# A hand-written order of a mixer's first inverses: chunks 0 and 1 first, convolutions in single steps

## The reference, cut to what matters

```python
S = S * w_t + sa (x) (kk_t * a_t) + v_t (x) k_t      # sa = S @ -kk_t; per token, 8 heads of 64
y = S @ r_t                                          # rwkv7_step, scanned over 512 tokens
...
xc = conv_b + sum(xp[:, i:i+seqlen] * conv_w[i] for i in range(4))
r, i_g = sigmoid(blocks(xc) @ gate_a_w + b), sigmoid(blocks(xc) @ gate_x_w + b)
a = exp(-8 * r * softplus(-lam)); u = sqrt(1 - a*a) * i_g * xc
h = scan(a, u); out = h * gelu(gb)                   # rglru_mix, 4 tiles of 128 channels
```

## Time and profile before

| | us |
|---|---|
| median of 3 runs | 3383.71 (3383.62 to 3385.1) |
| the profiled execution | 3382.94 |
| its span | 3381.2 |
| TensorE busy | 3325.3 (98%) |
| VectorE busy | 1982.3 (59%) |
| ScalarE busy | 1378.0 (41%) |
| GpSimd busy | 30.2 (1%) |

### The profile page before, as it was taken

One profiled execution on the slowest core, in us unless ns is written; L12 is line 12 of the kernel. 1 busy time (PEld: TensorE's weight loads), 2 busy tenths in 40 slices (PEclk: granted clock), 3 DMA queues, 4 the chain that ended last, 5 costly groups with the idle time before them and its releaser, 6 DMA issues.

```text
span 3381.2 us, 44358 instructions
## 1 busy us (share of the span) xinstructions
PE 3325.3 (98%) x18719; PEld 2691.3 (80%) x18719; DVE 1982.3 (59%) x2907; ACT 1378.0 (41%) x2111; POOL 30.2 (1%) x68
## 2 busy tenths in 40 slices
PE   8999999999999999999999999999999999999998
PEld 7888878888888888885788888657888887588887
DVE  6554687675546653436564435576765366676644
ACT  4332367443324332336543322365543243654433
POOL 0000003000000000000000000000000000000000
PEclk9999999999999999999999999999999999999999
DMA  5444430244443432220122223201223232023221
GB/s 199 144 144 148 132 119 3 94 148 140 142 150 125 157 111 94 90 100 32 38 94 98 96 99 144 69 32 57 98 97 100 92 143 69 13 82 105 95 100 56
DMA packets 93079, 342.32 MB, mean 101 GB/s; under 512 B 10320, under 2 KB 10832, under 8 KB 92368
## 3 DMA queue, kind: packets, MB, share of 16 engines
q1 hardware_dynamic: 92880, 339.48, 30.1%
HBM read 337.34 MB, written 2.10 MB: 100 GB/s over the span
## 4 chain that ended last, share of the span: by engine, by line
PE 89%; DVE 6%; ACT 4%; issue 1%; DMA 0%; POOL 0%; SPq 0%; DVEq 0%; ACTq 0%; POOLq 0%
PE ps L812 21%; PE ps L813 21%; PE ps L814 21%; PE ps L917 2%; PE ps L918 2%; PE ps L921 2%; PE ps L966 1%; PE ps L968 1%; PE ps L967 1%; PE ps L942 1%; PE ps L943 1%; PE ps L944 1%; ACT WK L2211 1%; DVE SPL L2320 1%; PE ps L1514 1%; ACT SPH L1607 1%
## 5 line engine op out<-in xcount | busy, mean ns | idle before, releaser
L2320 DVE TENSOR_TENSOR SPL<-RAW,SPH 128x1024 fp32r<-128x1024 f32 x522 | 635.6, 1223 | 876.6 <-ACT SPH L1607 876.2
L1607 ACT ACTIVATE SPH<-RAW 128x1024 fp32r<-128x1024 f32 x522 | 548.2, 1056 | 974.2 <-PE ps L814 867.4
L812 PE MATMUL ps<-HH,SPH 128*128 128x512 f32 x2312 | 910.2, 394 | 3.1 <-ACT WK L2138 1.9
L814 PE MATMUL ps<-HH,SPL 128*128 128x512 f32 x2312 | 900.2, 389 | 0.0
L813 PE MATMUL ps<-HL,SPH 128*128 128x512 f32 x2312 | 900.2, 389 | 0.0
L812 PEld LDWEIGHTS ps<-HH,SPH 128*128 128x128 f32 x2312 | 434.0, 188 | 104.8 <-issue 11.1
L813 PEld LDWEIGHTS ps<-HL,SPH 128*128 128x128 f32 x2312 | 434.1, 188 | 92.2 <-issue 3.6
L814 PEld LDWEIGHTS ps<-HH,SPL 128*128 128x128 f32 x2312 | 434.0, 188 | 90.7
L812 PE MATMUL ps<-AH,SPH 128*128 128x512 f32 x996 | 389.1, 391 | 0.7 <-DVE AH L2672 0.7
L814 PE MATMUL ps<-AH,SPL 128*128 128x512 f32 x996 | 387.7, 389 | 0.0
L813 PE MATMUL ps<-AL,SPH 128*128 128x512 f32 x924 | 359.6, 389 | 0.0
(11 more groups left out here) (570 smaller groups left out, 4335.2 us busy)
## 6 DMA issues: line engine op xcount, KB each, us to landing
RAW<-in_ws SPq DMA_DIRECT2D x522, 512.0 KB, 3.3
RAW<-in_wa SPq DMA_DIRECT2D x96, 512.0 KB, 3.5
WK<-in_sm SPq DMA_DIRECT2D x2, 2784.0 KB, 9.9
WK<-in_cst SPq DMA_DIRECT2D x2, 1664.0 KB, 7.5
X<-in_x SPq DMA_DIRECT2D x8, 256.0 KB, 8.2
out<-X SPq DMA_DIRECT2D x8, 256.0 KB, 2.7
WK<-in_sm SPq DMA_DIRECT2D x1, 768.0 KB, 4.9
PCT<-in_pc SPq DMA_DIRECT2D x1, 349.0 KB, 2.7
```

Of the source, the lines that this page charges most:

```text
L812: e.matmul(out, wh, rhs[0], start=start, stop=False)
L814: mm = e.matmul(out, wl, rhs[0], start=False, stop=stop)
L1607: e.activation(SPH[:, q:q + 1024], RAW[:, r:r + 1024], ACT.Copy).then_inc(hi_ready.did(("hi", n)))
L2320: e.tensor_tensor(SPL[:, q:q + 1024], RAW[:, r:r + 1024], SPH[:, q:q + 1024].bitcast(F32), ALU.subtract).then_inc(lo_ready.did(("lo", n)))
```

## The change

Chunk 0's `w0` moves from GpSimd to VectorE, as the new branch `w0`; the other three stay on GpSimd, chunk 1's now ahead of the memsets `t64`. On TensorE two `lt` are made first, then the values' transposes `vt` (before: after `nm` 3,3), then the first `nm` of chunks 0 and 1, with the other two `lt` between. `tr` 0 takes the place where `vt` was. `conv` takes a list of steps, and the three steps of tiles 0 and 1 stand as single items between the levels; tile 1's come behind tile 0's. On ScalarE `vtc` and `tanh` 0 move ahead, `gelu` behind `tanh` 0, and `bonb` behind `sq` 0; `kt` 0 and `bt` 0 move to where `vtc` was. The items behind those shown are as they were.

```diff
--- before.py
+++ after.py
@@ -196,14 +196,14 @@
 BONUS_SUMS_AT, BONUS_AT = {12: 0, 15: 1, 18: 2, 21: 3}, {13: 0, 16: 1, 19: 2}
 
 
-MIX0_TENSOR = [("01", "lt", 1), ("23", "lt", 0), ("45", "lt", 3), ("67", "lt", 2), ("23", "tr", 0),
-               ("0", "nm", 0, 1), ("1", "nm", 1, 1), ("23", "MK", 0, 1), ("67", "gates", 0), ("1", "dd", 1, 1),
-               ("0", "dd", 0, 1), ("45", "MK", 0, 0), ("2", "nm", 2, 1), ("3", "nm", 1, 2), ("1", "nm", 0, 2),
-               ("0", "dd", 2, 1), ("6", "dd", 1, 2), ("7", "dd", 0, 2), ("2", "nm", 3, 1), ("43", "gates", 1),
-               ("1", "nm", 1, 3), ("5", "dd", 3, 1), ("0", "nm", 0, 3), ("6", "dd", 1, 3), ("7", "nm", 3, 2),
+MIX0_TENSOR = [("01", "lt", 1), ("23", "lt", 0), ("4567", "vt"), ("0", "nm", 0, 1), ("1", "nm", 1, 1),
+               ("23", "lt", 2), ("0", "dd", 0, 1), ("1", "dd", 1, 1), ("45", "lt", 3), ("67", "MK", 0, 1),
+               ("1", "nm", 0, 2), ("3", "nm", 1, 2), ("0", "dd", 0, 2), ("45", "gates", 0), ("1", "dd", 1, 2),
+               ("2", "nm", 2, 1), ("3", "dd", 2, 1), ("2", "nm", 3, 1), ("67", "MK", 0, 0), ("1", "nm", 1, 3),
+               ("43", "gates", 1), ("5", "dd", 3, 1), ("0", "nm", 0, 3), ("6", "dd", 1, 3), ("7", "nm", 3, 2),
                ("2", "dd", 0, 3), ("1", "nm", 2, 2), ("5", "dd", 3, 2), ("3", "nm", 1, 4), ("40", "RB", 0),
                ("67", "MK", 1, 0), ("2", "nm", 0, 4), ("1", "dd", 2, 2), ("5", "dd", 1, 4), ("3", "dd", 0, 4),
-               ("2", "nm", 3, 3), ("1653", "vt"), ("2", "dd", 3, 3), ("6", "nm", 2, 3), ("3", "nm", 0, 5),
+               ("2", "nm", 3, 3), ("16", "tr", 0), ("2", "dd", 3, 3), ("6", "nm", 2, 3), ("3", "nm", 0, 5),
                ("51", "r0B", 0), ("6", "nm", 1, 5), ("2", "dd", 0, 5), ("3", "dd", 1, 5), ("4", "nm", 3, 4),
                ("6", "nm", 0, 6), ("2", "dd", 3, 4), ("43", "gates", 2), ("", "r0A", 0), ("62", "gates", 3),
                ("7", "nm", 3, 5), ("0", "yA", 0), ("34", "tr", 1), ("15", "nd", 1, 0), ("7", "dd", 2, 3),
@@ -218,11 +218,12 @@
                ("2", "yA", 3), ("6", "sap", 3), ("5", "fmean", 2), ("04", "tr", 3), ("7", "out", 0), ("3", "sp", 3),
                ("6", "fvar", 2), ("", "yp", 3), ("5", "out", 1), ("0", "fmean", 3), ("4", "fg", 3), ("3", "out", 2),
                ("6", "fvar", 3), ("2", "out", 3)]
-MIX0_VECTOR = [("LB", 1), ("LB", 0), ("conv", 1), ("LB", 2), ("w", 0, 0), ("LB", 3), ("w", 1, 0), ("conv", 0),
-               ("nmc", 1, 1), ("nmc", 0, 1), ("MKm", 0, 1, 0), ("MKm", 0, 1, 1), ("w", 2, 0), ("wt", 1, 1),
-               ("wt", 0, 1), ("w", 1, 1), ("w", 3, 0), ("w", 0, 1), ("nmc", 2, 1), ("MKm", 0, 0, 0), ("nmc", 1, 2),
-               ("nmc", 0, 2), ("MKm", 0, 0, 1), ("wt", 2, 1), ("iu", 0), ("wt", 1, 2), ("wt", 0, 2), ("w", 1, 2),
-               ("w", 2, 1), ("w", 0, 2), ("nmc", 3, 1), ("nmc", 1, 3), ("gm2", 0), ("wt", 3, 1), ("w", 3, 1),
+MIX0_VECTOR = [("LB", 1), ("LB", 0), ("w0", 0), ("w", 0, 0), ("w", 1, 0), ("conv", 0, 1), ("nmc", 0, 1),
+               ("nmc", 1, 1), ("LB", 2), ("wt", 0, 1), ("w", 0, 1), ("wt", 1, 1), ("w", 1, 1), ("LB", 3),
+               ("conv", 0, 2), ("conv", 0, 3), ("nmc", 0, 2), ("nmc", 1, 2), ("w", 2, 0), ("MKm", 0, 1, 0),
+               ("MKm", 0, 1, 1), ("wt", 0, 2), ("w", 0, 2), ("wt", 1, 2), ("w", 1, 2), ("nmc", 2, 1), ("w", 3, 0),
+               ("conv", 1, 1), ("conv", 1, 2), ("wt", 2, 1), ("w", 2, 1), ("conv", 1, 3), ("nmc", 3, 1),
+               ("nmc", 1, 3), ("MKm", 0, 0, 0), ("MKm", 0, 0, 1), ("iu", 0), ("gm2", 0), ("wt", 3, 1), ("w", 3, 1),
                ("nmc", 0, 3), ("wt", 1, 3), ("iu", 1), ("nmc", 3, 2), ("w", 1, 3), ("wt", 0, 3), ("hy", 0),
                ("w", 0, 3), ("nmc", 2, 2), ("gm2", 1), ("wt", 3, 2), ("nmc", 1, 4), ("nmc", 0, 4), ("w", 3, 2),
                ("wt", 2, 2), ("MKm", 1, 0, 0), ("wt", 1, 4), ("wt", 0, 4), ("w", 1, 4), ("w", 0, 4), ("nmc", 3, 3),
@@ -236,10 +237,11 @@
                ("RBm", 2, 1), ("ml", 2), ("RBm", 2, 0), ("ml", 3), ("RBm", 3, 0), ("RBm", 3, 1), ("state", 3),
                ("ylo", 1), ("hl", 22), ("fy", 2), ("hl", 23), ("hl", 24), ("hl", 25), ("fn", 2), ("ylo", 2),
                ("fy", 3), ("fn", 3), ("ylo", 3)]
-MIX0_SCALAR = [("xc", 0), ("xc", 1), ("gelu", 0), ("gelu", 1), ("ltm", 0), ("ltm", 1), ("kt", 0), ("bt", 0),
-               ("ltm", 2), ("ltm", 3), ("tanh", 0), ("bonb", 2), ("bonb", 3), ("bonb", 1), ("bonb", 0), ("gelu", 2),
-               ("gelu", 3), ("p2", 0), ("tanh", 1), ("sq", 0), ("p2", 1), ("xc", 2), ("sq", 1), ("vtc", 1),
-               ("vtc", 3), ("vtc", 2), ("vtc", 0), ("xc", 3), ("nmc", 0, 5), ("nmc", 1, 5), ("w5", 0), ("w5", 1),
+MIX0_SCALAR = [("xc", 0), ("xc", 1), ("ltm", 1), ("ltm", 0), ("vtc", 0), ("vtc", 1), ("vtc", 2), ("vtc", 3),
+               ("ltm", 2), ("ltm", 3), ("tanh", 0), ("gelu", 0), ("gelu", 1), ("gelu", 2),
+               ("gelu", 3), ("p2", 0), ("tanh", 1), ("sq", 0), ("bonb", 2), ("bonb", 3), ("bonb", 1), ("bonb", 0),
+               ("p2", 1), ("xc", 2), ("sq", 1), ("kt", 0),
+               ("bt", 0), ("xc", 3), ("nmc", 0, 5), ("nmc", 1, 5), ("w5", 0), ("w5", 1),
                ("nmc", 0, 6), ("tanh", 2), ("r0", 0), ("nmc", 3, 5), ("tanh", 3), ("nmc", 1, 6), ("p2", 2),
                ("sa", 0), ("p2", 3), ("sq", 2), ("sq", 3), ("w5", 3), ("nmc", 2, 5), ("mh", 1), ("yc", 0), ("kt", 2),
                ("bt", 2), ("r0", 1), ("nmc", 3, 6), ("sa", 1), ("bt", 1), ("w5", 2), ("kt", 1), ("fq", 0), ("mh", 0),
@@ -247,7 +249,7 @@
                ("mh", 3), ("mh", 2), ("yhi", 1), ("sa", 2), ("hh", 22), ("r0", 3), ("yc", 2), ("hh", 23), ("sa", 3),
                ("hh", 24), ("kt", 3), ("bt", 3), ("fq", 2), ("hh", 25), ("frs", 2, False), ("yc", 3), ("yhi", 2),
                ("fq", 3), ("frs", 3, False), ("yhi", 3)]
-MIX0_POOL = [("t64",), ("w0", 1), ("w0", 0), ("tt0",), ("w0", 2), ("w0", 3), ("wideT", 1), ("wideT", 0), ("wide", 0),
+MIX0_POOL = [("w0", 1), ("t64",), ("tt0",), ("w0", 2), ("w0", 3), ("wideT", 1), ("wideT", 0), ("wide", 0),
              ("wide", 1), ("wideT", 3), ("wide", 3), ("wideT", 2), ("wide", 2)]
 
 
@@ -2555,12 +2557,12 @@
                 w.wait_ge(("dm",), ("dex",))
                 e.tensor_tensor(DD[:, 0:15], DE[:, 0:15], DM[:, 1:16], ALU.mult).then_inc(dve_done.did(("prep_dd",)))
 
-                def lru(what, j):
+                def lru(what, j, *steps):
                     L = lru_places[j % 2]
                     if what == "conv":
                         x, xc = wk(XB[j]), L["U"]
-                        former = ("xc", j)
-                        for d in (1, 2, 3):
+                        former = ("conv", j, steps[0] - 1) if steps and steps[0] > 1 else ("xc", j)
+                        for d in steps or (1, 2, 3):
                             done = ("conv", j) if d == 3 else ("conv", j, d)
                             w.wait_ge(former)
                             e.scalar_tensor_tensor(xc[:, d:T], x[:, 0:T - d], pc("l0_conv_w", 4 * (3 - d) + j),
@@ -2610,6 +2612,14 @@
                             x = e.tensor_tensor(inv["LB"][c][:, 256 * hf:256 * hf + 256].rearrange("p (u x) -> p u x", u=4),
                                                 ps["lt", c, hf][:, 0:256].rearrange("p (u x) -> p u x", u=4), m, ALU.mult)
                         x.then_inc(dve_done.did(("LB", c)))
+                    elif what == "w0":
+                        v, wt = inv["LB"][c].rearrange("p (u x) -> p u x", u=8), u8(Wc[:, 256:512])
+                        w.wait_ge(("LB", c), ("bon", 3))
+                        e.tensor_tensor(wt, v[:, :, 0:32], v[:, :, 32:64], ALU.add).then_inc(dve_done.did(("w0a", c)))
+                        w.wait_ge(("w0a", c))
+                        e.tensor_tensor(wt, wt, b8(LV[:, 320:352]), ALU.mult).then_inc(dve_done.did(("w0b", c)))
+                        w.wait_ge(("w0b", c))
+                        e.tensor_tensor(wt, wt, b8(inv["DIAG"]), ALU.add).then_inc(dve_done.did(("wt", c, 0)))
                     elif what == "nmc":
                         w.wait_ge(("nm", c, lv), *([("dd", c, lv - 1)] if lv > 1 else []))
                         b = ps["nm", c, lv][:, 0:256].rearrange("p (u o x) -> p u o x", u=8, o=1)
@@ -2676,7 +2686,7 @@
                 for what, *x in MIX0_VECTOR:
                     if what in ("conv", "iu", "gm2", "hy", "ml"):
                         lru(what, *x)
-                    elif what in ("LB", "nmc", "w", "wt"):
+                    elif what in ("LB", "nmc", "w", "wt", "w0"):
                         inverse(what, *x)
                     elif what == "w6":
                         inverse(what, *x)
```

## The result

| | before | after |
|---|---|---|
| median, us | 3383.71 (5 runs, 3381.97 to 3385.1) | 3397.31 (5 runs, 3394.23 to 3401.31) |
| profiled execution | 3382.94 | 3394.23 |
| its span | 3381.2 | 3392.5 |

The ratio is 1.0038, interval 1.0027 to 1.0049: 13.6 us slower, where I forecast 2.0 and gave the range up to 3389.5.

The account below looks back on a forecast made before the run. The prediction took TensorE, busy 98% of the span, as the bound. Its terms -0.1 + 2.2 - 0.8 + 0.7 = +2.0 us put the median at 3383.7 + 2.0 = 3385.7, with the range 3381.0 to 3389.5.

Parts of the forecast that it names:

- The front: TensorE's waits ahead of the first off-diagonal products: idle 1.0 instead of 3.7 us, and 3.0 more won if the clock holds.
- rival 1: The clock falls in front, around the 16 transposes: +5.0 us in all, 3388.7; chance 0.25.
- The wait of 0.75 for nm 2,1's mask: TensorE waits 0.75 us for VectorE's mask ahead of dd 2,1, counted within the 11.5 us to 534.3.
- gm2 0 directly behind iu 0: VectorE stands 3.65 us for ScalarE's p2 0, TensorE 3.8 ahead of nm 3,2; front's gain used up, -0.1.
- The second meeting: VectorE stands 2.4 us ahead of gm2 1, waiting for ScalarE's p2 1; dd 1,4 starts 2.2 us later.
- The clock in the new wait: Clock falls in TensorE's 3.8 us wait near 542, for 3.4 or 6.8 us; +0.7 taken into the sum.
- The rule on transposes: Skill's rule weighed for the 16 transposes in front: if they count for nothing, the clock falls there, with rival 1's sum.
- Rivals 2, 3 and 4: 2: clock holds in all waits, 3385.0 (0.12); 3: front's gain survives, 3378.8 (0.12); 4: no second meeting, 3382.8 (0.08).
- Slower by over 0.2%: The whole run slower by more than 6.8 us; chance 0.05.
- a third loss beside rival 1: What the prediction said a slowdown of over 0.2% would take, a further loss added to rival 1.

Follow-up runs that it names:

- the run with MK 0,0 first: The changed kernel with the MK 0,0 products set ahead of dd 2,1 on TensorE, no work added; 3392.28 us, ratio 1.0028.
- the kernel with the front alone: The kernel before, TensorE's order kept, with chunk 0's start on VectorE, ScalarE's block copies ahead of gelus, GpSimd's starts ahead of memsets; 3380.45 us, ratio 0.9987.

## Why the prediction was wrong, point by point

- *The front*: right in kind. It says 1.0 us of idle; 1.71 came (VectorE's three instructions took 0.43 and 0.83 twice beside GpSimd, 2.16 in all where I had 1.45), with clock 1.00 up to 533 in the profiled execution. In others it falls there (rival 1, given 0.25): the profiled executions of five variants had it between 518.2 and 518.9.
- *The wait of 0.75 for nm 2,1's mask*: forecast, and 0.79 came. I took it as time and asked nothing of it for the clock. The clock fell 2 us behind it (533.3), and no longer there once the wait was filled. So the place was wrong as well as the length: I had the fall in the wait near 542.
- *gm2 0 directly behind iu 0*: right in kind and size (3.65 forecast, 3.67; TensorE's wait 3.8 forecast, 4.12 in the run with MK 0,0 first). In the changed kernel it is hidden by the slow clock and costs nothing.
- *The second meeting* (+2.2): VectorE waits 1.39 us and not 2.4, and it costs TensorE nothing, which is late from the clock. All waits of TensorE together went down by 0.9 us.
- *The clock in the new wait*: the step that failed. The text said "for 3.4 or 6.8 us, and TensorE loses 1.2 to 3.4", and put +0.7 into the sum, beside a front that had won its 3.0 back. Measured: 23.9 and 6.8 us at half clock, and 12.0 us more lost to it than before. I read the lengths from the three falls of the kernel before and didn't ask what ended them. In the earlier trace rows the first of them can be read: behind L1191 at 524.19, the wide MK 0,1, and the gates right behind it, the clock is back. The change moves these two apart, and that was to be seen in the diff.
- *The rule on transposes*: the Trainium skill ("TensorE: Matmul & The Clock Gate", "Part 4: PE-mode transpose") says that transposes don't count as activity as matmuls do, and so speaks against them in front. With the wide products apart, the clock came back right behind these 16 transposes, 3.58 us at half clock with no wait beside them (575.27), where small products had left it down; there the trace goes against the rule, and the measurement decides. In front, the fall after the 16 transposes and a wait of 1.7 us occurs in some executions and not in others, and three wide products in that wait take 6 us off the median. Whether the transposes have a part in it or the wait alone isn't shown.
- *Rivals 2, 3 and 4*: none came.
- *Slower by over 0.2%*, given 0.05, is what happened. I had thought that it takes a third loss beside rival 1; the clock staying down was enough.

What stays open: which executions fall in front and which later, and why a wide pair ended some low stretches and passed without effect in the three longest (58.0, 64.9 and 75.1 us). Falls and returns don't keep to the same place in the program, so one profile shows one draw; only the medians above weigh the variants. The exact mix of widths that brings the clock back wasn't measured by itself.

## What to carry to other kernels

Where TensorE runs small products, look in its timeline at durations of the same group before and behind each wait, however small, and keep wide products next to the places where it waits. In this stage closely placed wide products were worth more than the few microseconds that a tighter order won, though they are a help and no guarantee. When a diff scatters work by kind, price the clock over the whole stretch up to the next wide pair, and time many executions, as a single one may be on either side.

## What the runs showed of the hardware that I had not expected

- TensorE stayed at 1.2 GHz for 64.9 and 75.1 us though it was busy without a gap, with groups of 32-column products, single wide ones and one pair of wide ones (RB 0 and MK 1,0) in them.
- Moving wide products apart, with nothing added, cost 21 us in 3384.
- 16 fp32 transposes that filled 3.58 us at half clock were followed by the full clock at once.
- A fall came 2 us behind a wait of 0.79 us among such products, in other places in or behind 1.61 or 4.12 us. In the kernel with the front alone the clock held at 1.00 through waits of 1.79 and 0.55 us, so the length of a wait doesn't tell.
- It came back as four or six added products of 384 columns ran (4.23 and 6.07 us), in both profiles in which they were met at half clock.
- Two executions of one program differ by up to 23 us (3383.6 and 3406.9), with mean clocks of 0.997 and 0.988; the kernel before did so in one session too, 3381.1 and 3403.7.
